# Paged keys and paged values as two streams with places of their own in a hybrid decoder step

## What is computed

```
k_past = cache_k[page_table[b]]      # 32 pages of 128 x 512 floats, for each of 8 samples
v_past = cache_v[page_table[b]]
s = concat(q . k_past, q . k_new) / 8      # 4 heads x 2 components
p = softmax(s);  a = p[component 0] - lam * p[component 1]
o = a . concat(v_past, v_new)              # (4 heads x 128)
```

## Time and profile before

| | us |
|---|---|
| median of 3 runs | 1836.41 |
| lowest, highest | 1836.27, 1844.69 |
| the profiled execution | 1839.37 |
| its span in the trace | 1837.7 |
| PE busy | 1513.6 (82% of the span) |
| DVE busy | 803.0 (44%) |
| bytes moved | 598.58 MB, mean 326 GB/s |

### The profile page before, as it was taken

One profiled execution on the slowest core, in us unless ns is written; L12 is line 12 of the kernel. 1 busy time (PEld: TensorE's weight loads), 2 busy tenths in 40 slices (PEclk: granted clock), 3 DMA queues, 4 the chain that ended last, 5 costly groups with the idle time before them and its releaser, 6 DMA issues.

```text
span 1837.7 us, 32590 instructions
## 1 busy us (share of the span) xinstructions
PE 1513.6 (82%) x11928; PEld 606.2 (33%) x11929; DVE 803.0 (44%) x1184; ACT 332.8 (18%) x778; POOL 132.3 (7%) x201
## 2 busy tenths in 40 slices
PE   3869964667788985789999999899989998999970
PEld 2433321334433343233332333233323323333320
DVE  3698777887677225332131223213222312332325
ACT  2111111222121001011121121212112221212120
POOL 0000020000000002400000000001000000100100
PEclk8989985667888875789999999999999999999995
DMA  9368887777987653197999999999999999999975
GB/s 332 119 210 293 276 284 260 252 238 230 294 270 246 232 220 128 41 370 324 412 428 407 405 423 419 396 405 428 416 399 405 424 413 398 427 407 411 428 324 238
DMA packets 127874, 598.58 MB, mean 326 GB/s; under 512 B 20935, under 2 KB 20981, under 8 KB 102618
## 3 DMA queue, kind: packets, MB, share of 16 engines
q1 hardware_dynamic: 109088, 560.72, 77.9%
q10 hardware_dynamic: 8522, 20.00, 3.1%
q0 software_dynamic: 10208, 17.11, 2.5%
HBM read 589.89 MB, written 25.90 MB: 335 GB/s over the span
## 4 chain that ended last, share of the span: by engine, by line
PE 37%; DMA 20%; issue 1%; DVE 1%; SPq 0%; ACT 0%; DVEq 0%; ACTq 0%
PE bank L1410 23%; DMA wts<-in_w_gate_up 15%; PE bank L1447 7%; DMA wts<-in_w_down 4%; PE bank L1429 4%; DMA wts<-y_rows 1%; PE bank L1400 1%; PE bank L1496 1%; PE bank L1458 1%; DVE v_ring L2002 0%; DMA h_tok<-h_rows,v_tok 0%; ACT k_T L1064 0%; SPq L567 0%; SPq L578 0%; DVE qk L1949 0%
## 5 line engine op out<-in xcount | busy, mean ns | idle before, releaser
L1410 PE MATMUL bank<-wts,h_T 128*32 128x512 f32 x4096 | 463.0, 598 | 14.2 <-issue 6.9
L1948 DVE TENSOR_SCALAR q_T<-bank 128x512 f32<-128x512 f32 x32 | 22.1, 691 | 652.5 <-PE bank L1410 652.5
L1410 PEld LDWEIGHTS bank<-wts,h_T 128*32 128x32 f32 x4096 | 134.7, 111 | 326.6 <-issue 313.6
L1447 PE MATMUL bank<-wts,k_T 128*32 128x512 f32 x2048 | 230.5, 599 | 9.2 <-issue 6.2
L1536 DVE TENSOR_TENSOR wts<-wts,q_b 128x1024 f32<-128x1024 f32 x128 | 157.9, 1233 | 87.9 <-DMA wts<-in_cache_k 81.6
L1429 PE MATMUL bank<-wts,h_T 128*32 128x512 f32 x1024 | 131.3, 651 | 52.7 <-DMA wts<-in_w_gate_up 50.9
L1539 DVE TENSOR_REDUCE sc<-wts 128x16 f32<-128x1024 f32 x128 | 156.1, 1220 | 4.4
L1054 ACT ACTIVATE h_T<-bank 128x512 f32<-128x512 f32 x66 | 35.9, 595 | 585.2 <-PE bank L1400 585.2
L1447 PEld LDWEIGHTS bank<-wts,k_T 128*32 128x32 f32 x2048 | 67.0, 111 | 150.3 <-issue 138.6
L1378 PE MATMUL bank<-v_ring,ex 128*8 128x512 f32 x512 | 94.2, 730 | 14.6 <-DMA v_ring<-in_cache_v 14.6
L1125 PE MATMUL bank<-wts,h_T 128*8 128x128 f32 (+1 forms) x480 | 90.5, 459 | 14.9 <-DVE u_tok L1536 7.5
(11 more groups left out here) (299 smaller groups left out, 1384.0 us busy)
## 6 DMA issues: line engine op xcount, KB each, us to landing
wts<-in_w_gate_up SPq DMA_DIRECT2D x128, 2048.0 KB, 13.8
wts<-in_w_down SPq DMA_DIRECT2D x64, 2048.0 KB, 18.2
wts<-in_cache_k SPq DMA_DIRECT2D x256, 256.0 KB, 3.4
v_ring<-in_cache_v SPq DMA_DIRECT2D x256, 256.0 KB, 3.4
wts<-in_w_in SPq DMA_DIRECT2D x5, 2048.0 KB, 24.1
wts<-y_rows SPq DMA_DIRECT2D x4, 2048.0 KB, 15.2
wts<-in_w_out ACTq DMA_DIRECT2D x1, 4096.0 KB, 17.0
x_in<-in_x_prompt ACTq DMA_DIRECT2D x6, 512.0 KB, 5.4
```

Source lines behind the costliest of these rows:

```text
L1410: m = nc.tensor.matmul(PS[part][p0:p0 + 32, :], lhs[:, 32 * b:32 * b + 32], rhs[:, part * F + half * 512:part * F + half * 512 + 512], sta ...
L1447: m = nc.tensor.matmul(PS[4][p0:p0 + 32, :], act_T[0][:, k, a0:a0 + 32], chunk[c][:, k, n * 512:(n + 1) * 512], start=(c == 0 and k == 0), ...
```

## The change

Keys and values become two streams. `SCHEDULE` entries carry two weights, one for key steps and one for value steps, and `run_with_samples` keeps two counters. Key steps hold only the scores, of sample b; value steps hold the soft-max and the value products. Four things follow from the tables and the code:

- Key steps keep nearly the places they had (55 before Q begins, in both kernels). Value steps get none in P; they begin at Q(0). By Q's end 54 to 56 groups of values are done (before: 68 to 70), and 18 of 128 are left after R(2), where the remaining steps are put in one after another (before: none).
- Keys may lead values by up to four samples, so `sc` has four buffers (`LEAD`). The stages of the soft-max are spread over steps 0 to 12 instead of 1 to 8, and value products begin in step 7.
- Values get eight places (`VRING`): four in `v_ring` and four in `wts` slot 2, which was idle between the end of P and the first expert's chunk 0. That chunk is now loaded last of the four, when all values have been used. The new value row's buffer `v_new` is laid over `u_tok`.
- SP's page loads are no longer loops: SP walks `SCHEDULE` too, and each load is written out, with constants in its waits and page numbers.

```diff
-        V_LAG = 3
-        V_START = 5
+        V_START = 6
         V_OF_STEP = {V_START + g: (g - 1, g) if g % 2 else () for g in range(NG)}
-        def run_with_samples(step, stages):
-            steps = ((b, g) for b in range(-1, NB + 1) for g in range(NG if b < NB else V_START))
+        def run_with_samples(key_step, value_step, stages):
+            keys = ((b, g) for b in range(NB) for g in range(NG))
+            values = ((b, g) for b in range(NB + 1) for g in range(NG if b < NB else V_START))
+            due = {key_step: 0, value_step: 0}
+            for part, k, v in SCHEDULE:
                 if part:
                     next(stages[part], None)
+                for step, steps, weight in ((key_step, keys, k), (value_step, values, v)):
+                    due[step] += weight
+                    while due[step] >= 1:
...
-        plan(("V", 0), *[2.4] * (CT + 1))
+        plan(("V", 0), *[1.6] * (CT + 1), values=2.4)
...
-                plan(("R", s), 1.25 if s == 1 else 1.75)
+                plan(("R", s), 1, values=1)
...
-        SCHEDULE.append((None, STEPS_ALL))
+        SCHEDULE.append((None, ALL, ALL))
...
+        v_more = w_slot[2].rearrange("p (s g n) -> p s g n", s=RING, g=GP)
+        def v_of(m):
+            return (v_ring if m % VRING < RING else v_more)[:, m % RING]
...
-            def load_pages(ring, full, cache, used, first_page, r, need):
-                if need is not None:
-                    sp.wait_ge(used, need)
-                sp.load(page_regs, pages_sb[0:1, bass.ds(first_page, GP)])
+            def load_group(dst, done, cache, n):
+                sp.load(page_regs, pages_sb[0:1, n * GP:(n + 1) * GP])
...
-                        with sp.Fori(2 * half, 2 * half + 2) as four:
-                            for r in range(RING):
-                                if not last:
-                                    load_k(b + 1, four, r)
-                                load_v(b, four, r)
+            def load_keys(n):
+                after(sp, kred_done, n + 1 - RING)
+                load_group(k_ring[:, n % RING], k_full[n % RING], kc, n)
+            def load_values(m):
+                if m == RING:
+                    k, n = filled(a_full, a_no[("P", TILES)][4])
+                    sp.wait_ge(k, n)
+                after(sp, pv_done, m + 1 - VRING)
+                load_group(v_of(m), v_full[m % VRING], vc, m)
...
-            load_chunk(0, 0)
             sp.wait_ge(fold_done, 2 * CT)
             for c in range(1, 3):
                 load_chunk(c, 0)
             sp.wait_ge(kred_done, NB * NG)
             load_chunk(3, 0)
+            sp.wait_ge(pv_done, NB * NG)
+            load_chunk(0, 0)
```

More of the change, by code:

```diff
@@ L23 @@
 RING = 4
+VRING = 8
+LEAD = 4
 IN_COLS = 2560
@@ L205, in hybrid_step, with plan @@
         UNITS = H * TILES
-        STEPS_ALL = 1 << 20
+        ALL = 1 << 20
         SCHEDULE = []
-        def plan(part, *weights):
-            SCHEDULE.extend((part, w) for w in weights)
+        def plan(part, *weights, values=0):
+            SCHEDULE.extend((part, w, values) for w in weights)
         plan(("P", 0), *[0] * 9)
@@ L452, in load_q @@
[L452 to L466, removed]
@@ L468, in step @@
-            def step(b, first=False, last=False):
-                for half in range(2):
-                    if first and half == 0:
-                        for four in range(2):
-                            for r in range(RING):
-                                load_k(b + 1, four, r)
-                                if four or r >= V_LAG:
-                                    load_v(b, four, r, wait=four * RING + r - V_LAG >= RING)
-                    else:
-                        with sp.Fori(2 * half, 2 * half + 2) as four:
-                            for r in range(RING):
-                                if not last:
-                                    load_k(b + 1, four, r)
-                                load_v(b, four, r)
-                    if half == 0:
-                        if not first:
-                            sp.wait_ge(u_all, b)
-                        sp.dma_start(v_new[0:1, :], new_v_rows[0][bass.ds(b, 1), :]).then_inc(vn_in, 16)
@@ L504, in _ @@
-            step(NB - 1, last=True)
-            for r in range(V_LAG):
-                load_v(NB, 0, r)
+                    sp.dma_start(dst[:, p, :], cache[bass.ds(page, 1)].rearrange("a p n -> (a p) n")).then_inc(done, 16)
+            def load_keys(n):
[7 more added lines that the diff above has]
+                load_group(v_of(m), v_full[m % VRING], vc, m)
@@ L509, in load_chunk @@
+            for n in range(RING):
+                load_keys(n)
+            sp.wait_ge(sample_rows_out, 64)
+            load_q(0)
+            load_q(1)
+            run_with_samples(key_step, value_step, {part: iter(()) for part in a_no})
             def load_chunk(c, e):
@@ new lines, in value_step @@
+            def value_step(b, g):
+                if b == NB:
+                    return
+                scores = sc[:, b % LEAD, :, :]
+                if g == 0:
+                    if b == 0:
+                        dve.wait_ge(sn_in, 16)
+                    V.link(nc.vector.tensor_copy(sc[0:1, b % LEAD, PAGES, :], s_new[0:1, b * HC:(b + 1) * HC]))
+                    dve.wait_ge(kred_done, NG * (b + 1))
+                    after(dve, small_pe, 3 * b - 2)
+                    nc.vector.tensor_reduce(pmax[:, :], scores.rearrange("p g e -> p e g"), X, ALU.max
+                                            ).then_inc(pm_done, 1)
+                if g == 2:
```

194 lines of the change are left out of this document (96 added, 98 removed).

## The result

| | before | after |
|---|---|---|
| median, us | 1836.57 (4 runs) | 1791.15 (4 runs) |
| ratio, 95% interval | | 0.975 [0.9712, 0.9788] |
| span of the profiled execution, us | 1837.7 | 1788.1 |
| first expert begins on PE, us | 747.3 | 693.7 |

The account below looks back on a forecast made before the run. The front was taken to set the change, paced by SP's 1.88 us per group in Q, V, L. Terms: P - 21, Q to L - 17, R and W - 3, block + 20 = - 21 us: 1815 us, range 1794 to 1842.

Parts of the forecast that it names:

- the part on Q, V and L: Q's start to L's end, 306 us before: transfers would bind at 289 us, a gain of 17.
- the four others: Bounds priced below transfers in Q, V, L; three are listed: SP 246 us, PE 229, DVE 215 plus about 4.
- 247 + 33 = 280 us: Q, V, L: transfers' earlier busy share times length, plus 22 more groups at 1.48 us each, at full share.
- SP's 246 us: Q, V, L: SP's time to issue 159 groups at 1.55 us each.
- The eight value places instead of four are what lets SP run on: Q, V, L: more places let SP keep issuing; their price was eight loads, 12.4 us, before further keys at Q's start.
- P, - 28.8 for - 21: Stretch before Q, 155 us: value work leaves and DVE's 15.5 us of key waits go, giving 134, a gain of 21.
- R and W, - 11.0 for - 3: Stretch after L, 77 us: value groups fall from 26 to 20, key groups rise from 4 to 12; 74, gain 3.
- The block: After R(2): 18 value groups with no other work, ten still to issue; 20 us lost, ends 12 and 34.
- The tail: Last stretch before the experts: keeps its 102 us, as the chunk now issued last still comes in time.
- Slow transfers: Rival: DMA share stays at 0.83 in Q, V, L, which take 337 us; total 1863, chance 0.17.
- Unchanged pitch: Rival: SP's written-out loads still take 1.88 us a group; Q to L 305 us, total 1835, chance 0.10.
- The cold clock: Rival: value products moved from P to Q's slower PE clock add 14.5 us; total 1830, chance 0.12.

Follow-up runs that it names:

- e3: Changed kernel with the page numbers of four groups of a stream read by one register load; ratio to before 0.9635, Q to L 256.4 us.
- e10: Changed kernel at its own pitch, loading only half of each page's columns after the first eight groups of each stream; ratio to before 0.9682, Q to L 266.2 us.
- e11: Changed kernel with half of each page's columns loaded and one register load per four groups' page numbers; ratio to before 0.9587, Q to L 252.4 us.
- e1: Kernel before, with SP's page loads written out instead of looped, order and waits unchanged; ratio to before 0.9864, Q to L 288.9 us.
- e12: Changed kernel with four value places instead of eight, each load at the step whose products free its place; ratio to before 0.9839, Q to L 282.1 us.
- e7: Changed kernel with four value places instead of eight, loads two steps after the products freeing their place; ratio to before 1.0134, Q to L 318.8 us.
- e6: Changed kernel with higher key and value weights in R and W, so no values are left after R(2); ratio to before 0.9715.
- e5: Kernel before, with the first expert's gate-up chunks issued only after all loads of x for the residual sums landed; ratio to before 0.9949.
- e2: Repeat of the changed kernel: the intended second register load was not in the program that ran; ratio to before 0.9728, Q to L 269.8 us.
- e9: Changed kernel with each page number read by its own register load, two per group; ratio to before 0.9766, Q to L 277.6 us.

## Why the prediction was wrong

**The step that failed** is in the part on Q, V and L: "So the transfers now bind, ahead of the four others", with its 247 + 33 = 280 us as the least possible time at a full share. The stretch took 270.0 us, and 256.4 with the same bytes in e3. Three things were wrong in it.

- A busy share is not a capacity. I multiplied share by length and kept the product as work. Before, 79.75 MB took 0.81 x 303 = 245 us of it, 325 GB/s; after, 88.97 MB took 0.96 x 270 = 259, 343 GB/s; in e3 it is 353. The median value load took 3.4 us from issue to landing before, 4.2 after and 5.3 in e3 (265 to 500 us), so more loads were under way at once, and the same bytes took less busy time. By e3's rate the transfers' floor is 252 us, not 280; by the 387 GB/s of e3's best 30 us it is lower still. The prediction had such a rate in hand: it priced the added groups at 346 GB/s for a share of 0.98, which is 353 for a share of one, and left the groups that were there at 325.
- The count. The order gave 22 more groups, 137 before and 159 after; by the issues in the stretch it was 18 (139 before, 157 after), as loads run ahead of their use. That is 33 us taken for 27.
- The bound itself. The two by two of e3, e10 and e11 shows that transfers were not what set 270 us: 4 us for 44% of the bytes, 14 for the page numbers' register loads. SP's 246 us, which I had computed and set aside as the smaller number, was nearer: 157 x 1.55 = 243 us of issue and 17.6 of waits are 261 of the 270; the other 9 us hold SP's nine other transfers and are not split further.

e3 and e11 add that SP's is no hard bound either: at 1.2 us a group SP waits 56 us, DVE is full in the part of Q shown above, and the stretch takes 252 to 256 us.

The misses partly cancel. The measured terms add up to 49.5 us less, the forecast ones to 21. From Q to L 16 us more were gained than forecast, in the tail 10, in P and in R and W 8 each; against these stand 9 us more for the block and 4 in the expert loop. That the sum is not further off is luck: the miss in the block hides part of the others.

**Where the 33 us come from.** Written-out loads alone give 13.8 (e1). Two streams with four places take it from 288.9 to 282.1 with 16 more groups issued inside (e12), eight places to 270.0. In the step to e12 the order, the lead of the keys and the higher count of groups are not separated. No one of these steps does it: e1 spends 29 us in new waits for places, and e7 shows streams with four badly placed loads to be 16 us worse than before. The prediction's "The eight value places instead of four are what lets SP run on" had no price; e12 gives it, 12 us. Its mechanism is half right: in one sequence with four places SP does wait for PE (62.2 us, e1), but in two streams with four it hardly does (3.7), and it is PE that waits for values (33.8 us, for 13.5 with eight).

**P, - 28.8 for - 21.** The mechanism was right: key waits of 15.5 us are gone from DVE's list, whose longest wait in 107 to 236 us is now

```profile
DVE qk L1543 <- ACT stp L765: 5.2, 3, 1.7
```

Three of the missing 8 us are my cut (262, where Q's first scores stand at 265.15); DVE is busy 117.6 us, not 119.7, and idle 11.4, not 14.1. In e1 P took 150.9 us: faster issue alone gives 7.2 of the 28.8; the rest came with the value work's leaving.

**R and W, - 11.0 for - 3.** Undersized. e1 has 80.8 us here, so 1.9 come with the pitch; the other 9 go with six fewer value groups and their waits, not separated further.

**The block, + 28.8 for + 20.** The place and the mechanism were right. By the trace 20 groups of values are multiplied behind R(2)'s last product, two of them still of its last step by the order. SP around that product, at 577.95 us:

```profile
570.08 7.12 SPq L462 DMA_DIRECT2D v_ring<-in_cache_v  x8
584.88 6.31 SPq L462 DMA_DIRECT2D wts<-in_cache_v  x8
591.89 2.46 SPq L462 DMA_DIRECT2D v_ring<-in_cache_v  x4
...
598.75 5.52 SPq L462 DMA_DIRECT2D wts<-in_cache_v  x8
604.33 1.38 SPq L520 DMA_DIRECT2D wts<-in_w_gate_up  x3
```

I had ten groups issued from R(2)'s end on. It was 12, in 19.4 us, but SP stood from 577.2 to 584.9 because no place came free: PE had to spread the maximum (581.52) and use the ready groups first. These 7 us are the term I did not have; the two further groups are another 4, the end after the last group's issue took 6 us and not 4.4, and I had not taken off the 3.7 us that stood there before. How much of the block is a loss stays open: e6 took it away and the front ended at the same time, but with the wait for x back in the tail.

**The tail, - 9.8 for 0.** I argued only that the chunks would be in time for the experts, and did not ask what else they delay. The load of x into `rot` waited behind 8 MB; the row was in the trace. Moving the chunks behind it gave 6.6 us in e5; the rest of the 9.8 is not explained (in e2 the tail is 84.6 us, 8.5 less than before).

**The rivals.** Slow transfers (0.17) did not come: the share is 0.96. The Trainium skill's wish for batches of 1 MiB or more ("DMA: Bandwidth & Descriptors", section "Bandwidth") did not limit this kernel: 256 KB loads that are queued behind each other moved 346 GB/s over 257 us in e3. The measurement decides here. Unchanged pitch fell at once: 1.55. The cold clock did not come: with 20 more value groups multiplied from Q to L (90 for 70), PE's busy time went from 205.0 to 207.7 us where the prediction had 229, while the granted clock rose from 0.72 to 0.83 and PE's busy share of the stretch from 0.68 to 0.77. That activity lifts the granted clock, as the Trainium skill says ("TensorE: Matmul & The Clock Gate", section "Part 1: The HAM clock gate (the "warmup" mystery)"), agrees with these two figures: the moved work largely paid for itself.

## What to carry to other kernels

When an engine that only issues transfers is never idle, count its instructions before trusting a DMA share: a share near one says that the queues are fed, not that fewer bytes would help. Bytes per busy time changed here with the pace of issue; as a bound for transfers, take the best rate seen in the trace and not the average one. Where a load stands in the issuing engine's list can cost more than the number of places (37 us for 12). And when a burst of large loads moves, look for the small loads behind it: the wait went away with the block and came back without it.

## What the runs showed of the hardware

- SP's issue of one page load depends on its form: four of 128x512 in 2.40 us, four of 128x256 in 2.43, four of 64x512 in 2.97: half the rows cost more than the whole page.
- A register load of two page numbers costs SP 0.5 us: groups without one stand 1.05 us apart (e3, 293.78 to 294.83 us) and with one 1.55. The load itself takes 0.27 us for one number (e9), 0.47 for two, 0.53 for eight (e3). Two loads of one number cost 0.6: transfer follows transfer at 0.82 us there, at 0.52 without a load.
- 2 KB rows in 256 KB transfers: 325, 343 and 353 GB/s per unit of busy share from Q to L, as the pitch falls from 1.88 to 1.55 and to e3's 1.2. For 30 us of e3 it was 387 GB/s at a share that the view gives as 1.05.
